# RWKV features in 30 turns, one for each 128 features of a stage, between those of latent attention

## The chip, the core and the metric

The kernel runs on one core of a Trainium2 chip. The metric is the device time of one execution in microseconds; three executions of the kernel before took 3229.11, 3230.69 and 3238.85 us, median 3230.69. Five engines work at once, each on its own queue of instructions in program order: PE (TensorE: matrix products and transposes), DVE (VectorE), ACT (ScalarE), POOL (GpSimd) and SP (SyncE, which issues the DMAs). They wait for each other only through semaphores written out in the code.

## The reference

Two blocks of two layers each on 512 tokens of width 1024, all in float32. The first block (sliding window, forgetting and mLSTM mixers, squared ReLU) is not touched. A layer of the second block computes three mixers from one projection: stick-breaking attention, latent attention (MLA, 4 heads) and RWKV-7 (8 heads of 64, 512 features), then an output projection, a norm, a feed-forward part with a short convolution, and a norm. The change lies in what the RWKV mixer does before its recurrence:

```
kk = (k * k_k).reshape(b, s, RWKV_HEADS, HEAD_DIM)
kk = kk * lax.rsqrt(jnp.maximum(jnp.sum(jnp.square(kk), axis=-1, keepdims=True), 1e-12))
k = k * (1.0 + (a - 1.0) * k_a)
...
def step(state, inp):
    sa = jnp.einsum('bhvk,bhk->bhv', state, -kk_t)
    state = (state * w_t[:, :, None, :] + sa[..., None] * (kk_t * a_t)[:, :, None, :]
             + v_t[..., None] * k_t[:, :, None, :])
    return state, jnp.einsum('bhvk,bhk->bhv', state, r_t)
...
bonus = jnp.sum(rh * kh * r_k, axis=-1, keepdims=True) * vh
```

## The kernel before

**The mixer stage.** In each of the two RWKV layers, after the input projection, all engines run the same set of strands by `turns`: each strand is a generator, and one turn calls each of them once, in the order `latent`, `stick`, `strand(2)`, `strand(3)`, `features`, `prep(0)` to `prep(3)`, `scan`, `post(0)` to `post(3)`. What a strand issues in its part of a turn goes to the engine's queue in that order. Each engine has its own generators with the same names, and their `yield`s are counted so that the same step falls into the same turn on every engine. Nothing waits at the end of a turn; a turn only fixes the order in each queue. Order between strands is set by `flags`: a strand that finds its flag missing yields and asks again next turn. A fence of all engines ends the stage, and the output projection follows.

**The strands.** `latent` makes queries and keys of latent attention and sets `mla`. `strand(2)` and `strand(3)` then work through four attention units each (`attend`, L637, L1378, L2061; 512, 384, 256, 128 keys wide, two heads each): scores on PE in a unit's turn 0, mask and maximum on DVE in 1, the negated maximum in 2, exponentials on ACT in 3, transposes on PE and their copies in 4, products with the values in 5, the scaled output on DVE in 6, so seven turns for a unit. `features` (PE L893, DVE L1703, ACT L2235, POOL L2523) makes what the recurrence needs from receptance, key, value, decay and rate, which lie as features x tokens in four chunks of 128 features by 512 tokens (`rF`, `kF`, `vF`, `KKv`, `AAv`). Its first two turns (rates and decay projections) come when stick-breaking ends; the rest when `mla` is set, in these steps, each for all four chunks in one turn: cumulative log decays (PE) and their exponentials `E1v`, `E2v` (ACT); squares of the gained key (ACT) summed by head with `Oblk` (PE); clamp at 1e-12 (DVE); reciprocal root as ln, exp (ACT) and one Newton step (DVE); values turned to tokens (PE, ACT); norm of the key, gate by `ka`, bonus operand (DVE); `AAv` times key and `E2v` (POOL); the bonus sums with `hsel` (PE); decayed key and receptance (DVE); key, normed key and rate turned (PE, copied by ACT or DVE to `KT`, `AT`, `BT`). In banks 0 to 3 of PSUM chunk c always uses bank c.

**After the features.** `prep(t)` (PE L962) inverts a triangular matrix for each tile of 128 tokens by five levels of 64x64 products and takes 17 turns on PE; `prep(0)` and `prep(1)` wait for `feat`, `prep(2)` and `prep(3)` also for the end of both attention strands (`gates_of`, L474), whose PSUM banks and buffers they use. `scan` carries the state from tile to tile. `post(t)`, the group norm, bonus and gate of a tile, waits for the states of its pair of tiles and the end of attention (`gates_post`).

In the trace nearly all DVE, ACT and POOL operations stand on lines of small helpers: L1204 tensor_tensor, L1208 and L1209 tensor_scalar, L1212 scalar_tensor_tensor, L1215 reduce, L1943 activation, L1939 activation with a sum, L2449 POOL tensor_tensor; L519 is a product and L522 a transpose of PE, L989 and L1039 products inside `prep`. Buffers are slices of larger ones: R, SC, HA and LN hold the mixer's tensors, RAW the attention scores, PS is PSUM, PSM the parameters by feature. `own(x)` issues x and waits on the engine for its end.

## Time and profile before

| | |
|---|---|
| median of three runs | 3230.69 us (3229.11 to 3238.85) |
| the profiled execution: whole time, span | 3235.39 us, 3233.6 us |
| mean granted clock of PE, as a share of 2.4 GHz | 0.916 |
| PE, DVE, ACT, POOL busy | 2880.6, 1547.8, 1044.6, 191.7 us |
| share of the span | 89%, 48%, 32%, 6% |
| DMA | 216.59 MB, 67 GB/s in the mean |

Busy time is the time in which an engine has an instruction at work. A share near 90% for PE says that the kernel as a whole is bound there, not that each stage is: the mixer stages of the second block last from 1618.5 to 1843.2 us and from 2543.7 to 2773.0 us (counted from the first scores of latent attention to the end of the mixer), and there it has to be read stage by stage. The granted clock is the share of full speed that PE was given in a stretch; its two levels are 1.2 and 2.4 GHz, so 0.72 means a mixture of both. In a timeline row stand start, length, engine, line, operation, out<-in with shapes, the count of instructions merged in it, and in brackets how long the engine had been idle and for whom.

### The profile page before, as it was taken

Reading aid. Unit: us, or ns where it says so; the run is one execution under the profiler, and the core shown is the slowest. Engines: PE = TensorE matmul, PEld = TensorE weight load, DVE = VectorE, ACT = ScalarE, POOL = GpSimd, SP = SyncE. Lnnn points to the kernel's source line nnn. Section 1 sums busy time; section 2 is a strip of 40 time slices with the busy share of each in tenths; the row PEclk is TensorE's granted clock in tenths of the full one; section 3 lists DMA queues with packets and bytes.
Section 4 is the critical chain, followed back from the end, with each engine's and each line's share of the span. In section 5 each row is a group of like instructions: output and inputs, shape, how many; then the busy total and the mean of one; then the engine's idle time right before and its main releaser. Section 6 shows DMA issues by size and latency. Waiting matters only on the chain.

```text
span 3233.6 us, 45203 instructions
## 1 busy us (share of the span) xinstructions
PE 2880.6 (89%) x19896; PEld 2379.5 (74%) x19896; DVE 1547.8 (48%) x2432; ACT 1044.6 (32%) x1554; POOL 191.7 (6%) x182
## 2 busy tenths in 40 slices
PE   7987999999888999998867789999888687789997
PEld 5876788878777888886557678888666387678885
DVE  3585533345565443424365554444533555554435
ACT  3333322232333322224232233223433432232323
POOL 0200000001100000000023200000000123000000
PEclk9977999999868999999878889999898798889998
DMA  4101222222003222221000123232210000223221
GB/s 163 53 1 62 80 103 94 102 78 84 9 1 108 99 98 98 89 86 40 1 1 29 51 89 108 92 104 78 84 52 1 1 3 29 92 78 104 91 98 46
DMA packets 30725, 216.59 MB, mean 67 GB/s; under 512 B 3648, under 2 KB 3776, under 8 KB 6080
## 3 DMA queue, kind: packets, MB, share of 16 engines
q1 hardware_dynamic: 30528, 213.69, 18.8%
q8 instruction: 157, 2.57, 0.3%
q14 instruction: 40, 0.33, 0.0%
HBM read 211.58 MB, written 2.10 MB: 66 GB/s over the span
## 4 chain that ended last, share of the span: by engine, by line
PE 80%; DVE 14%; ACT 4%; issue 2%; DMA 0%; DVEq 0%; SPq 0%; ACTq 0%
PE PS L519 76%; PE PS L522 3%; DVE SC L1204 2%; DVE SM L1215 1%; DVE X L1204 1%; DVE SM L1204 1%; DVE R L1204 1%; ACT LN L1943 1%; ACT SPL L1943 1%; DVE SPL L1204 1%; DVE HA L1204 1%; PE PS L1039 0%; PE PS L989 0%; ACT R L1943 0%; DVE SM L1209 0%
## 5 line engine op out<-in xcount | busy, mean ns | idle before, releaser
L519 PE MATMUL PS<-H,SPL 128*128 128x512 f32 (+1 forms) x4560 | 1056.4, 392 | 8.7 <-DVE SPL L1204 5.6
L519 PEld LDWEIGHTS PS<-H,SPL 128*128 128x128 f32 (+1 forms) x4560 | 853.5, 188 | 194.8 <-issue 8.2
L1204 DVE TENSOR_TENSOR SPL<-RAW,SPL 128x2048 fp32r<-128x2048 f32 (+2 forms) x194 | 434.3, 2240 | 768.3 <-ACT SPL L1943 768.3
L1943 ACT ACTIVATE SPL<-RAW 128x2048 fp32r<-128x2048 f32 (+2 forms) x194 | 362.0, 1869 | 922.4 <-PE PS L519 888.2
L519 PE MATMUL PS<-SPL,Uu 128*128 128x512 f32 x2592 | 589.8, 389 | 0.0
L519 PEld LDWEIGHTS PS<-SPL,Uu 128*128 128x128 f32 x2592 | 486.5, 188 | 101.0
L519 PE MATMUL PS<-SPL,H 128*128 128x512 f32 (+2 forms) x2112 | 463.6, 381 | 25.7 <-DVE SPL L1204 25.0
L519 PEld LDWEIGHTS PS<-SPL,H 128*128 128x128 f32 x2112 | 389.3, 193 | 99.4 <-issue 27.1
L1943 ACT ACTIVATE R<-PS 128x512 f32<-128x512 f32 (+2 forms) x182 | 104.6, 585 | 267.9 <-PE PS L519 243.1
L1204 DVE TENSOR_TENSOR X<-X,PS 128x512 f32<-128x512 f32 x112 | 76.7, 685 | 116.0 <-PE PS L519 116.0
L1943 ACT ACTIVATE Uu<-R 128x512 fp32r<-128x512 f32 x108 | 68.3, 632 | 141.2 <-DVE R L1204 141.2
L1204 DVE TENSOR_TENSOR Uu<-R,Uu 128x512 fp32r<-128x512 f32 x108 | 74.8, 693 | 79.8 <-ACT Uu L1943 79.8
L1204 DVE TENSOR_TENSOR R<-R,PS 128x512 f32<-128x512 f32 (+1 forms) x86 | 57.6, 670 | 105.5 <-PE PS L519 90.1
L519 PEld LDWEIGHTS PS<-R,SC 64*64 64x64 f32 (+1 forms) x1280 | 89.8, 182 | 19.7 <-issue 12.4
L522 PE MATMUL PS<-CST,R 128*128 128x128 f32 (+1 forms) x384 | 63.5, 332 | 41.3 <-DVE R L1208 23.4
L519 PE MATMUL PS<-R,SC 64*64 64x64 f32 (+1 forms) x1280 | 96.7, 269 | 2.4 <-ACT SC L1943 1.9
L519 PE MATMUL PS<-SM,CST 128*128 128x128 f32 (+5 forms) x224 | 61.9, 428 | 35.1 <-DVE SM L1204 35.1
L522 PEld LDWEIGHTS PS<-CST,R 128*128 128x128 f32 (+1 forms) x384 | 56.2, 173 | 49.2 <-issue 15.5
L1204 DVE TENSOR_TENSOR LN<-LN,PS 128x512 f32<-128x512 f32 (+3 forms) x74 | 42.5, 578 | 92.7 <-PE PS L519 92.6
L519 PE MATMUL PS<-R 64*64 64x64 f32 (+2 forms) x1760 | 71.7, 235 | 16.3 <-DVE R L1204 9.5
L519 PEld LDWEIGHTS PS<-SM,CST 128*128 128x128 f32 x224 | 44.1, 238 | 56.7 <-DVE SM L1204 37.9
L2449 POOL TENSOR_TENSOR HA<-HA,CST 128x64 f32<-128x64 f32 x16 | 4.6, 322 | 1313.4 <-ACT HA L1943 1313.4
(220 smaller groups left out, 2704.5 us busy)
## 6 DMA issues: line engine op xcount, KB each, us to landing
RAW<-in_wA SPq DMA_DIRECT2D x84, 1024.0 KB, 4.8
RAW<-in_wB SPq DMA_DIRECT2D x84, 1024.0 KB, 4.8
RAW<-in_wAo SPq DMA_DIRECT2D x8, 1024.0 KB, 4.8
RAW<-in_wBo SPq DMA_DIRECT2D x8, 1024.0 KB, 6.3
LN<-in_ln SPq DMA_DIRECT2D x4, 1024.0 KB, 6.1
P<-in_pB SPq DMA_DIRECT2D x2, 1920.0 KB, 8.9
RAW<-in_wBm SPq DMA_DIRECT2D x4, 704.0 KB, 4.1
X<-in_x SPq DMA_DIRECT2D x4, 512.0 KB, 5.0
```

Of the source, the lines that this page charges most:

```text
L519: return pe.matmul(out, l_, r_, start=start, stop=stop)
L522: return pe.transpose(out, i, C("ident"))
L1204: return v.tensor_tensor(out, a, b, o)
L1215: return v.tensor_reduce(out=out, in_=a, op=o, axis=AX.X)
L1943: return a.activation(out, in_, f, scale=scale)
L2449: return g.tensor_tensor(out, a, b, o)
```

## The change

After `mla` the features' steps run one chunk in a turn. Each step for all four chunks, one turn long before, becomes four turns long; the seven turns of PE after `mla` become 28, and with the two earlier ones 30. The strands on DVE, ACT and POOL get the same number of turns, with idle ones where they have nothing to do. `flags["feat"]` is set at the end of the 28th turn after `mla` on every engine, in the same turn as the last output of attention's fourth unit.

The gained key (`kF` times `kk`) is no longer written to `KKv` beforehand by four DVE operations. ACT squares `kF` with `kk` as its scale, and the norm multiplies `kF`, `kk` and the reciprocal root in one scalar_tensor_tensor. The Newton step is three operations there, not four: y times (1.5 - 0.5 x y y) is formed with two scalar_tensor_tensor and one tensor_tensor. So DVE has four operations up to the normed key in each chunk where it had five. The counts of the semaphore `fe_d` go down from 16 to 12 in a layer.

```diff
@@ -912,36 +912,38 @@
                         ins = mm(bank(c)[:, t * 128:(t + 1) * 128], LW[:, t * 512 + c * 128:t * 512 + (c + 1) * 128],
                                  C("Ublk"))
                     ins.then_inc(s.fe_p, 1)
-                yield
+                    yield
                 for c in range(4):
                     pe.wait_ge(s.fe_e, 12 * l + 4 + c + 1)
                     mm(bank(c), C("Oblk"), FT[c][0]).then_inc(s.fe_r, 1)
-                yield
+                    yield
                 for c in range(4):
-                    pe.wait_ge(s.fe_d, 16 * l + 4 + c + 1)
+                    pe.wait_ge(s.fe_d, 12 * l + c + 1)
                     turned(c, vF, c, s.fe_t)
-                yield
+                    yield
                 for c in range(4):
                     pe.wait_ge(s.fe_c, 12 * l + c + 1)
-                    pe.wait_ge(s.fe_d, 16 * l + 8 + c + 1)
+                    pe.wait_ge(s.fe_d, 12 * l + 4 + c + 1)
                     for t in range(4):
                         ins = mm(bank(c)[:, t * 2:t * 2 + 2], FT[c][0][:, t * 128:(t + 1) * 128], C("hsel"))
                     ins.then_inc(s.fe_r, 1)
-                yield
+                    yield
                 for c in range(4):
                     pe.wait_ge(s.fe_k, 8 * l + c + 1)
                     turned(c, kF, c, s.fe_t)
-                yield
+                    yield
                 for c in range(4):
                     pe.wait_ge(s.fe_c, 12 * l + 4 + c + 1)
                     pe.wait_ge(s.fe_k, 8 * l + 4 + c + 1)
                     turned(c, KKv, c, s.fe_r)
-                yield
+                    yield
                 for c in range(4):
-                    pe.wait_ge(s.fe_d, 16 * l + 12 + c + 1)
+                    pe.wait_ge(s.fe_d, 12 * l + 8 + c + 1)
                     pe.wait_ge(s.fe_g, 4 * l + c + 1)
                     turned(c, AAv, c, s.fe_t)
-                pe.wait_ge(s.fe_d, 16 * l + 16)
+                    if c < 3:
+                        yield
+                pe.wait_ge(s.fe_d, 12 * l + 12)
                 pe.wait_ge(s.fe_c, 12 * l + 12)
                 flags["feat"] = True
                 yield
@@ -1704,9 +1706,6 @@
                 while "sb" not in flags:
                     yield
                 v.wait_ge(s.par, 16 * (3 + l))
-                for c in range(4):
-                    ts(KKv[:, c, :], kF[:, c, :], par(PS, PSM, f"kk_{l}", c, c + 1), None, ALU.mult,
-                       None).then_inc(s.fe_d, 1)
                 yield
                 for t in range(4):
                     v.wait_ge(s.fe_p, 8 * l + t + 1)
@@ -1714,40 +1713,45 @@
                 yield
                 while "mla" not in flags:
                     yield
-                yield
+                for c in range(4):
+                    yield
                 for c in range(4):
                     v.wait_ge(s.fe_r, 12 * l + c + 1)
                     ts(FT[c][0], bank(c), 1e-12, None, ALU.max, None).then_inc(s.fe_d, 1)
-                yield
+                    yield
                 for c in range(4):
                     T1_, T2_, T3_ = FT[c]
                     v.wait_ge(s.fe_e, 12 * l + 8 + c + 1)
-                    own(newton(T2_, T1_, T3_))
-                    own(tt(KKv[:, c, :], KKv[:, c, :], T2_, ALU.mult))
+                    own(stt(T3_, T2_, -0.5, T2_, ALU.mult, ALU.mult))
+                    own(tt(T3_, T3_, T1_, ALU.mult))
+                    own(stt(T2_, T3_, 1.5, T2_, ALU.add, ALU.mult))
+                    own(stt(KKv[:, c, :], kF[:, c, :], par(PS, PSM, f"kk_{l}", c, c + 1), T2_, ALU.mult, ALU.mult))
                     v.wait_ge(s.rw_a, 4 * l + c + 1)
                     own(ts(T1_, AAv[:, c, :], -1.0, par(PS, PSM, f"ka_{l}", c, c + 1), ALU.add, ALU.mult))
                     own(stt(kF[:, c, :], T1_, 1.0, kF[:, c, :], ALU.add, ALU.mult))
                     stt(T1_, rF[:, c, :], par(PS, PSM, f"rk_{l}", c, c + 1), kF[:, c, :], ALU.mult,
                         ALU.mult).then_inc(s.fe_d, 1)
-                yield
+                    yield
                 for c in range(4):
                     v.wait_ge(s.fe_r, 12 * l + 4 + c + 1)
                     v.tensor_copy(BN.rearrange("p (t c g) -> p c t g", t=4, c=4)[:, c], v3(bank(c, 8), 4))
                     tt(kF[:, c, :], kF[:, c, :], E2v[c], ALU.mult).then_inc(s.fe_k, 1)
                     tt(rF[:, c, :], rF[:, c, :], E1v[c], ALU.mult)
                     v.tensor_copy(AC4[:, c, :].unsqueeze(2), E1v[c].rearrange("p (i s) -> p i s", s=64)[:, :, 63:64])
-                yield
+                    yield
                 for c in range(4):
                     e8 = E1v[c].rearrange("p (i s) -> p i s", s=64)
                     kk8 = KKv[:, c, :].rearrange("p (i s) -> p i s", s=64)
                     v.wait_ge(s.fe_h, 4 * l + c + 1)
                     tt(kk8[:, :, 1:64], kk8[:, :, 1:64], e8[:, :, 0:63], ALU.mult).then_inc(s.fe_k, 1)
-                yield
+                    yield
                 for c in range(4):
                     v.wait_ge(s.fe_r, 12 * l + 8 + c + 1)
                     v.tensor_copy(AT.rearrange("p (t c d) -> p c t d", t=4, c=4)[:, c],
                                   v3(bank(c), 4)).then_inc(s.fe_d, 1)
-                yield
+                    yield
+                for c in range(3):
+                    yield
                 flags["feat"] = True
                 yield
 
@@ -2231,6 +2235,7 @@
                     a.wait_ge(s.fe_t, k + c + 1)
                     act(dst.rearrange("p (t c d) -> p c t d", t=4, c=4)[:, c], v3(bank(c), 4),
                         ACT.Copy).then_inc(s.fe_c, 1)
+                    yield
 
             def features(l):
                 while "sb" not in flags:
@@ -2249,24 +2254,29 @@
                 while "mla" not in flags:
                     yield
                 for c in range(4):
-                    a.wait_ge(s.fe_d, 16 * l + c + 1)
-                    act(FT[c][0], KKv[:, c, :], ACT.Square).then_inc(s.fe_e, 1)
+                    act(FT[c][0], kF[:, c, :], ACT.Square,
+                        scale=par(PS, PSM, f"kk_{l}", c, c + 1)).then_inc(s.fe_e, 1)
                 for c in range(4):
                     a.wait_ge(s.fe_p, 8 * l + 4 + c + 1)
                     act(E1v[c], bank(c), ACT.Exp, scale=-DECAY)
                     act(E2v[c], bank(c), ACT.Exp, scale=DECAY).then_inc(s.fe_e, 1)
-                yield
-                yield
+                    yield
                 for c in range(4):
-                    a.wait_ge(s.fe_d, 16 * l + 4 + c + 1)
+                    a.wait_ge(s.fe_d, 12 * l + c + 1)
                     rsqrt0(FT[c][1], FT[c][0], FT[c][2]).then_inc(s.fe_e, 1)
-                turned(VT, 12 * l)
-                yield
-                yield
-                turned(KT, 12 * l + 4)
-                yield
-                yield
-                turned(BT, 12 * l + 8)
+                    yield
+                yield from turned(VT, 12 * l)
+                for c in range(4):
+                    yield
+                yield from turned(KT, 12 * l + 4)
+                for c in range(4):
+                    yield
+                for c in range(4):
+                    a.wait_ge(s.fe_t, 12 * l + 8 + c + 1)
+                    act(BT.rearrange("p (t c d) -> p c t d", t=4, c=4)[:, c], v3(bank(c), 4),
+                        ACT.Copy).then_inc(s.fe_c, 1)
+                    if c < 3:
+                        yield
                 flags["feat"] = True
                 yield
 
@@ -2527,17 +2537,16 @@
                 yield
                 while "mla" not in flags:
                     yield
-                yield
-                yield
+                for c in range(8):
+                    yield
                 for c in range(4):
-                    g.wait_ge(s.fe_d, 16 * l + 8 + c + 1)
+                    g.wait_ge(s.fe_d, 12 * l + 4 + c + 1)
                     tt(AAv[:, c, :], AAv[:, c, :], KKv[:, c, :], ALU.mult).then_inc(s.fe_h, 1)
                     g.wait_ge(s.fe_h, 4 * l + c + 1)
                     tt(AAv[:, c, :], AAv[:, c, :], E2v[c], ALU.mult).then_inc(s.fe_g, 1)
-                yield
-                yield
-                yield
-                yield
+                    yield
+                for c in range(15):
+                    yield
                 flags["feat"] = True
                 yield
 
```

## Rows read from the trace of the kernel before

**Rows 1.** The page: its first line, and section 4 by engine.

```profile
span 3233.6 us, 45203 instructions
...
PE 80%; DVE 14%; ACT 4%; issue 2%; DMA 0%; DVEq 0%; SPq 0%; ACTq 0%
```

**Rows 2.** Busy time by stage: start:end, length, PE, PEld, DVE, ACT, POOL (count), clock, DMA.

```profile
1618.50:1679.10 60.60, 35.80 (x192) 29.24 (x192) 45.86 (x72) 22.44 (x45) 13.05 (x8) 0.72 0.00 0
1679.10:1751.10 72.00, 64.83 (x1936) 60.29 (x1936) 32.53 (x66) 24.13 (x56) 21.39 (x18) 0.98 0.02 4
1751.10:1823.00 71.90, 54.31 (x1853) 51.58 (x1854) 38.65 (x62) 14.64 (x27) 27.95 (x22) 0.83 0.09 32
1823.00:1843.20 20.20, 6.09 (x116) 3.27 (x112) 15.50 (x31) 2.69 (x7) 4.90 (x4) 0.71 0.00 1
...
2543.70:2604.30 60.60, 35.67 (x195) 29.15 (x195) 45.86 (x72) 22.37 (x44) 13.06 (x8) 0.72 0.00 0
2604.30:2678.00 73.70, 65.53 (x1926) 60.30 (x1928) 32.22 (x64) 24.13 (x56) 21.43 (x18) 0.95 0.02 4
2678.00:2752.80 74.80, 57.41 (x1867) 54.35 (x1865) 39.35 (x64) 14.64 (x28) 27.95 (x22) 0.82 0.09 31
2752.80:2773.00 20.20, 6.12 (x117) 3.30 (x111) 15.49 (x31) 2.69 (x7) 4.91 (x4) 0.76 0.00 1
```

**Rows 3.** Timeline of DVE in a chunk of features; columns as told above.

```profile
1648.15 2.36 DVE L1204 TENSOR_TENSOR HA<-HA 128x512 f32<-128x512 f32 x2
1650.55 1.37 DVE L1209 TENSOR_SCALAR HA<-HA 128x512 f32<-128x512 f32 x1
...
1652.67 0.69 DVE L1204 TENSOR_TENSOR SC<-SC,HA 128x512 f32<-128x512 f32 x1
1653.40 0.48 DVE L1209 TENSOR_SCALAR HA<-SC,PSM 128x512 f32<-128x512 f32 x1
...
1654.65 0.75 DVE L1212 SCALAR_TENSOR_TENSOR HA<-R,PSM 128x512 f32<-128x512 f32 x1
```

**Rows 4.** Timeline of POOL in the same chunk, the first of its two.

```profile
1648.31 1.66 POOL L2449 TENSOR_TENSOR SC<-SC 128x512 f32<-128x512 f32 x1 [3.85 <-DVE HA L1212]
```

**Rows 5.** Timeline of PE from the first scores of latent attention on.

```profile
1618.57 5.40 PE L519 MATMUL PS<-SC 96*128 96x512 f32 x8 [4.20 <-ACT SC L1943]
1623.81 3.73 PE L519 MATMUL PS<-CST,R 128*128 128x128 f32 x32
...
1664.42 3.43 PE L522 MATMUL PS<-CST,RAW 128*128 128x128 f32 x16
...
1670.94 3.76 PE L519 MATMUL PS<-SC,RAW 128*128 128x64 f32 x32 [0.77 <-DVE RAW L1418]
...
1682.79 2.20 PE L519 MATMUL PS<-SC 96*128 96x384 f32 x6 [0.71 <-issue]
...
1695.08 1.10 PE L519 MATMUL PS<-HA,R 64*64 64x64 f32 x32
...
1751.11 2.09 PE L519 MATMUL PS<-SC 64*64 64x64 f32 x128
...
1778.15 1.92 PE L519 MATMUL PS<-HA,R 64*64 64x64 f32 x32
```

**Rows 6.** Timeline of DVE and of ACT, attention unit 1.

```profile
1630.19 1.22 DVE L1215 TENSOR_REDUCE SM<-RAW 128x2 f32<-128x1024 f32 x1
...
1640.54 0.74 ACT L1939 ACTIVATE RAW<-RAW,SM 128x512 f32<-128x512 f32 x1
```

**Rows 7.** Chain that ended last, preps 2 and 3 and post: start, length, what.

```profile
1782.99 29.64 PE PS L519 x960
...
1812.69 2.57 PE PS L989 x174
...
1819.25 3.72 PE PS L1039 x128
...
1840.27 2.09 PE PS L519 x2
```

## Prediction

> **What bounds the kernel now.** I read the page first. TensorE is busy for most of the span and the chain that ended last lies 80% on PE and 14% on DVE [rows 1]; the dense products are not touched, so what counts is the mixer stage of the two RWKV layers, the only place where the changed lines run. Then the table by stage [rows 2], cut at four events of the PE timeline: first scores of latent attention (1618.5), first pair products of the RWKV preps 0 and 1 (1679.1), those of preps 2 and 3 (1751.1), end of their last products (1823.0), end of the mixer (1843.2). I call the stretches I to IV. In I, 60.6 us, PE is busy 35.8 and DVE 45.9: the features hold everything up, one DVE chain after another. In II, 72.0 us, PE is busy 64.8: preps 0 and 1 and units 2 to 4 of attention share PE, and PE is the bound. In III, 71.9 us, PE is busy 54.3 at a mean clock of 0.83: only two preps run, and DVE is shared with the output steps (post) of tiles 0 and 1. In IV, 20.2 us, PE is nearly idle: scan, and post of tiles 2 and 3 on DVE. Sum 224.7 us in the first RWKV layer, 229.3 in the second.
>
> What sets these stretches is the turn in which a strand may start. Attention has 4 units of 7 turns on both of its strands, turns 0 to 27. Features now end in turn 6, so preps 0 and 1 (17 turns) run in 6 to 22 beside attention; preps 2 and 3 need the end of attention and run in 28 to 44.
>
> **The change part by part.**
>
> **DVE operations.** A chunk loses one operation of five in the norm of the keys (square, times sum, affine, times r, times key become four, and the multiply by the key gain is folded in). The row for the affine step undisturbed is not among the five; the tensor_scalar that gates the key took 0.48 [rows 3], so 4 x 0.48 = 1.9 us leave each layer's DVE chain. The four multiplies that made the gained key earlier stood under PE's and ACT's work before stretch I, where DVE had nothing to do; they are worth nothing, and if that cover were gone they would be 4 x 0.48 = 1.9 us.
>
> **The new turns.** Features take 28 turns after latent attention is open, 0 to 27, one 128-feature chunk in each. Attention ends in 27 as before. So preps 0 and 1 start in turn 27 and preps 2 and 3 in 28: all four together. Stretch II disappears as a stretch; the stage becomes A (turns 0 to 27: attention and features), B (27 to 44: four preps), C (scan and four posts). Posts need the states of both tiles of a pair: tiles 0 and 1 have them in turn 47, tiles 2 and 3 in turn 52, where now the first pair starts in 28 and the second in 48.
>
> *A, walked along the new order from 1618.5.* (1) To the first DVE norm chain. Scores 5.4 [rows 5], first cumulative product 0.9 (a quarter of 3.73, [rows 5]), then ACT does the exponentials of chunk 0 before it copies the scores, which queue behind that new wait: 1.8. DVE masks and reduces twice, 3.4 (1.22 each for the maximum, [rows 6]), ACT's exponentials 2.8 (4 at the 0.74 row, less their overlap, [rows 6]), transposes of the second strand 1.7 (half of 3.43, [rows 5]), sum product 0.9, value products 3.8 [rows 5], the next sum product 0.9 and the two outputs of the unit 1.1, scores of unit 2 between 2.2 and 4.4 (the row at full clock is 2.20, [rows 5]; twice that at half), I take 3.1, sum product, clamp, ln and exp, copy of the scores 3.6, small ones 0.7. Together 30.1. (2) Masks of unit 2, 2.8; four norm chains. One chain is now 4 x 0.69 + 0.75 x 2 + 0.48 plus gaps = 4.9 undisturbed [rows 3]. In the trace a chunk takes 7.2 (its last operation ends at 1655.4, that of the chunk before at 1648.2, [rows 3]), because its second and third operations wait for GpSimd's two multiplies (2.36 for two and 1.37, where alone they would take 0.69 each and about the 0.48 of the other tensor_scalar) [rows 3, 4]: 2.1 us lost in each. GpSimd still does the same two multiplies a chunk later, beside the next chunk's chain. No row has a scalar_tensor_tensor beside a GpSimd operation, so the loss is between 0 and 2.1, and could be a little more since a tiny maximum negation now stands first and waits as well; I take 2.1, as the nearest rows are tensor operations with two operands in SBUF like these. 4.9 + 3 x 7.0 + 1.5 + copies 0.9 + 2.8 = 31.1. (3) Bonus copies, decays of key and receptance, unit 3's mask, shifted keys: 16.4, DVE nearly all of it. (4) Values of unit 3, output, scores, mask, exponentials, transposes, values of unit 4 and the last turned copies: PE, DVE and ACT hand to each other, 13.9. A = 91.5, between 82 (no loss to GpSimd, -6.3, and PE at full clock, -3) and 99 (half clock throughout, +7).
>
> One rule of the Trainium skill speaks to the open price in (2): GPSIMD Engine Reference, section Specifications, says that GpSimd shares its SBUF interfaces with VectorE and collides with a VectorE operation that reads two SBUF operands, without an exception for a kind. By that the new operations lose as the old ones do (A near 91.5); by the lower end of the rows A would be 85.
>
> *B.* A prep on PE: the first products, 128 records of a pair in 2.09 [rows 5]; the second and third steps, 192 records at that pace, 2.8; the fourth, 128 records of which 32 step on by 0.94 (the row says 1.10 to their end, [rows 5]), 3.8; 960 records in 29.64; then 2.6, short ones of about 1.1, and 3.7 [rows 7]. That is 46.0 for a pair, 92.0 for four. Holes: at the start DVE has to mask for four preps (15 operations of 0.69 in the first turns, from the 0.69 row) and PE waits about 5; at the end about 2.5 (now 2.9: from 1815.3 to 1819.3 less the short ones, [rows 7]); and 1.5 for the half clock at the start. B = 101, between 96 and 106. DVE per level is 8 x 0.69 = 5.5 against PE's 11.9, GpSimd less: neither takes over. This is where the change gains: II and III are 143.9 now, A beyond I and B together 30.9 + 101 = 131.9, so 12.0 less.
>
> *C.* Scan needs tiles in order. Three steps remain after B (2.3), then post of tiles 0 and 1, then three scan adds (1.3), then post of tiles 2 and 3. A pair of posts alone is DVE after DVE and a last gate product of 2.09 at half clock [rows 7]: stretch IV less its scan, 16.7, and 17.1 with the one copy that tile 0 has. C = 37.7 against 20.2: 17.5 us more. Posts of tiles 0 and 1 are not free today, but PE fills much of their time in III; afterwards nothing is left to run beside them, since all preps are over. That is the price of the late features.
>
> **Sum.** A + B + C = 91.5 + 101 + 37.7 = 230.2 us per layer; now 224.7 and 229.3: +5.5 and +0.9, together +6.4 us. The profiled execution has a span of 3233.6 and a whole time of 3235.4, 4.7 above the median of 3230.7, within the shown runs; I put the difference on the median: 3237.
>
> **The rivals.**
>
> *Faster: the chunks fill the holes better than I walk it.* For it: stretch I has 24.8 us without PE work, III 17.6, and these are what the new order mixes. Against it: C. If the chains lose nothing to GpSimd (-6.3 per layer), PE stays at full clock in A (-3) and B has only 2 us of holes (-6), a layer is 214.9: -9.8 and -14.4, 3206.5; half way from my sum to it is 3222.
>
> *Slower: PE runs at its lower level through A.* In A PE is busy about half of the time, in bursts with idle stretches of up to 10 us. The trace has the pattern: III starts after a long idle of PE, its mean clock is 0.83, and 32 small products there take 1.92 where the same form in II, under continuous load at 0.98, takes 1.10 [rows 2, 5]. If the scores, transposes and values of units 1 to 4 all run at 1.2 GHz and the start of B too, +7 in A and up to +5 in B: a layer is 242.2, +17.5 and +12.9, 3261; half way to it from my sum is 3249. It decides against the change as soon as it costs more than 2 us per layer beyond my sum. The Trainium skill has this as its own warning, TensorE: Matmul & The Clock Gate, section on HAM oscillation: short products between waits lose the full clock again and again. The trace agrees (0.72 in I).
>
> *No effect where it is meant:* features could be bounded by attention's units anyway, and preps 2 and 3 are gated by the end of attention before and after. Then only the order of preps 0 and 1 and their posts moves, and gain in B and loss in C cancel: 3231. This is the middle of "same" and differs from my forecast by less than a measurement can tell.
>
> **How the numbers follow.** A measurement of this kernel tells about 0.3%, 9.7 us, from no change: the bounds are 3221 and 3240.4. My forecast with the no-effect case, 3221 to 3240: 0.41. Faster case: 0.24, two thirds of it between 3210 and 3221. Slower case: 0.35, two thirds of it up to 3252. The range that leaves 2 in 10 out is 3211 to 3254; it takes A between 82 and 99 nearly whole in both layers. The likeliest case's own range is 3221 to 3240.
>
> **What would show it.** In the new profile: the first pair products of preps 0 and 1 follow the values of attention's last unit, some 91 us after the first scores, and those of preps 2 and 3 come within 10 us after them. PE is busy over 90% of some 100 us from there. DVE's norm chain has four operations before the key, near 7 us a chunk when GpSimd runs. After the last prep products there are two runs of post, about 38 us to the end of the mixer, not 20. I am wrong if the chain beside GpSimd takes 5 us a chunk, if the clock in A is above 0.9 or below 0.6, if tile 0's post starts before the last prep ends, or if B has more than 10 us of idle PE.

## Result, and the profile of the changed kernel

The changed kernel takes 3260.04 us (median of 7 runs, 3248.08 to 3269.72), the kernel before 3235.11 us (7 runs, 3220.08 to 3239.17): ratio 1.0099, 95% interval 1.0071 to 1.0127. It is slower by 24.9 us. The forecast was 3237 with a range of 3211 to 3254: the result lies outside it. The profiled execution took 3267.71 us with a span of 3265.9, 32.3 more than that of before [rows 1].

The page of the changed kernel, its first line and section 4 by engine, which answer to [rows 1]:

```profile
span 3265.9 us, 45193 instructions
...
PE 81%; DVE 12%; ACT 4%; issue 2%; DMA 0%; DVEq 0%; SPq 0%; ACTq 0%
```

The table by stage of the changed kernel, both RWKV layers, cut where the prediction cut it: A from the first scores to the first pair products, B to the end of the last products of the preps, C to the end of the mixer. The columns are those of [rows 2]: start:end, length, PE, PEld, DVE, ACT, POOL, clock, DMA.

```profile
1621.50:1715.80 94.30, 61.26 (x288) 51.22 (x289) 54.54 (x100) 33.92 (x78) 12.35 (x8) 0.65 0.01 3
1715.80:1825.60 109.80, 96.78 (x3607) 94.96 (x3609) 44.26 (x65) 25.57 (x43) 44.02 (x36) 0.94 0.06 21
1825.60:1863.40 37.80, 14.16 (x202) 8.06 (x198) 30.71 (x62) 4.79 (x13) 10.05 (x8) 0.61 0.00 1
2564.00:2657.90 93.90, 60.61 (x288) 50.34 (x289) 54.55 (x100) 33.86 (x78) 12.36 (x8) 0.67 0.01 3
2657.90:2766.90 109.00, 96.53 (x3606) 94.86 (x3608) 44.13 (x65) 25.69 (x43) 43.95 (x36) 0.94 0.06 22
2766.90:2804.60 37.70, 14.51 (x200) 8.05 (x196) 30.70 (x62) 4.79 (x13) 10.05 (x8) 0.67 0.00 1
```

Beside the old stretches (I, II+III and IV in [rows 2]) and the forecast:

| us | I, II+III, IV before (layer 1; layer 2) | forecast A, B, C | after (layer 1; layer 2) |
|---|---|---|---|
| A | 60.6; 60.6 | 91.5 | 94.3; 93.9 |
| B | 143.9; 148.5 | 101 | 109.8; 109.0 |
| C | 20.2; 20.2 | 37.7 | 37.8; 37.7 |
| sum | 224.7; 229.3 | 230.2 | 241.9; 240.6 |

The two stages grew by 17.2 and 11.3 us, 28.5 of the 32.3 between the two profiled executions; 2.9 more lie ahead of the first scores, where of the change only the four removed VectorE multiplies stood; the first scores of the other profiled kernels come anywhere from 1599.5 to 1628.2 us, so this part is spread. So the place is right and C is right; A is 2.8 and 2.4 us too long, and B 8.8 and 8.0, which is most of the error.

The chain that ended last, in B of the changed kernel (start, length, what; "issue" is time in which PE waits for nothing that the profile shows):

```profile
1715.81 4.64 PE PS L519 x160
1720.45 1.47 issue
1721.92 3.45 PE PS L519 x124
1725.37 0.71 issue
1726.08 2.09 PE PS L519 x128
1728.17 1.91 issue
1730.09 2.09 PE PS L519 x127
1732.18 1.96 issue
1734.13 10.66 PE PS L519 x351
...
1799.77 2.09 PE PS L991 x128
1801.86 1.65 issue
...
1813.10 1.65 issue
```

Here stands the row from which the prediction made its price: 128 records in 2.09 us, the same as in [rows 5]. Behind such bursts stands what it left out, a pause of up to 2 us in which no engine is waited for. Eight such pauses on this chain in B add up to 10.9 us (the six shown, and 1.03 and 0.48 in the left-out part). Only one pause over 1 us in B has a releaser, 1.39 us for VectorE at 1744.77.

B of the changed kernel once more, cut into its levels (middle) and what lies behind and ahead of them:

```profile
1734.13:1799.77 65.64, 63.97 (x2168) 63.55 (x2169) 26.92 (x40) 16.72 (x28) 22.45 (x18) 0.97 0.02 4
1799.77:1825.60 25.83, 20.52 (x896) 19.68 (x898) 6.02 (x10) 6.46 (x11) 7.54 (x8) 1.00 0.02 4
1715.80:1734.13 18.33, 12.28 (x543) 11.74 (x543) 11.31 (x16) 2.39 (x4) 14.04 (x10) 0.75 0.27 107
```

Length by count gives 30.3 ns a record in the levels, 28.8 behind them, 33.8 ahead of them (where the clock is 0.75). The three are nearly alike, but not for the same reason. In the levels PE has hardly a pause: from 1747 to 1799 two products start every 59 ns, 29.5 ns for each. Outside them the 128 of a burst start 16 ns apart, and the pause makes up the rest. The levels of before had 960 in 29.64 us, 30.9 ns [rows 7].

### The profile page after: what moved, and what is told of

It reads as the page before. It is cut to its first block, busy times and chain, and to the rows that moved or that the text cites. A ratio compares the mean times of both kernels' runs of the same rounds, so it can differ in the third digit from the quotient of the medians.

```text
span 3265.9 us, 45193 instructions
## 1 busy us (share of the span) xinstructions
PE 2902.4 (89%) x19896; PEld 2399.8 (73%) x19896; DVE 1538.9 (47%) x2416; ACT 1045.9 (32%) x1554; POOL 189.8 (6%) x182
## 4 chain that ended last, share of the span: by engine, by line
PE 81%; DVE 12%; ACT 4%; issue 2%; DMA 0%; DVEq 0%; SPq 0%; ACTq 0%
PE PS L519 77%; PE PS L522 3%; DVE SC L1206 2%; DVE SM L1217 1%; DVE X L1206 1%; DVE SM L1206 1%; ACT SPL L1947 1%; ACT LN L1947 1%; DVE SPL L1206 1%; DVE R L1206 1%; PE PS L991 1%; DVE HA L1214 1%; PE PS L1041 0%; DVE X L1211 0%; DVE SM L1211 0%
## 5 line engine op out<-in xcount | busy, mean ns | idle before, releaser
L519 PE MATMUL PS<-SPL,H 128*128 128x512 f32 (+2 forms) x2112 | 462.7, 381 | 25.5 <-DVE SPL L1206 24.7
L519 PEld LDWEIGHTS PS<-R 64*64 64x64 f32 (+1 forms) x1760 | 63.1, 146 | 26.0 <-issue 12.8
```

The lines of the kernel that those rows point to most:

```text
L519: return pe.matmul(out, l_, r_, start=start, stop=stop)
```

## The experiments

A, B and C of a kernel are its stretches as in the table above, and of two numbers for one stretch the first is that of the first RWKV layer. Each stretch comes from one profiled execution. How far such a number can be trusted is seen where kernels share the lines of a stretch: A is 94.3 in the first layer and 93.6 to 93.9 in the second in the changed kernel and in three others with the same A, but B lies between 106.0 and 109.8 in four kernels with the same preps, and II+III between 143.5 and 148.5 in four with the old ones. So a difference of 2 or 3 us in B or in II+III tells nothing by itself.

**1. The two parts apart.** First the new operations in the old order of turns:

```diff
-                    own(newton(T2_, T1_, T3_))
-                    own(tt(KKv[:, c, :], KKv[:, c, :], T2_, ALU.mult))
+                    own(stt(T3_, T2_, -0.5, T2_, ALU.mult, ALU.mult))
+                    own(tt(T3_, T3_, T1_, ALU.mult))
+                    own(stt(T2_, T3_, 1.5, T2_, ALU.add, ALU.mult))
+                    own(stt(KKv[:, c, :], kF[:, c, :], par(PS, PSM, f"kk_{l}", c, c + 1), T2_, ALU.mult, ALU.mult))
```

> The kernel before with the new VectorE operations alone (no gained key beforehand, four operations up to the normed key where there were five); the turns are those of before. Theory (the cost lies in the order of the turns): stretch I of the layer, 60.6 us before, loses 4 x 0.45 to 4 x 0.75, that is 1.8 to 3 us, the rest stays, so 4 to 6 us less for the whole kernel, too little to be clear beside its spread. Rival (the new operations are the cost, because each waits longer beside GpSimd): stretch I grows, and the kernel is 10 us or more slower than before.

Measured: 3232.79 us beside 3230.64, ratio 1.0007 (0.9990 to 1.0025), no difference that can be told. Stretch I takes 59.0 and 59.4 us, 1.6 and 1.2 less than before, a little under the 1.9 of the prediction and the 1.8 expected at least; the whole layers take 226.1 and 225.9 where before has 224.7 and 229.3, no clear change.

Then the new turns with the old operations (the diff above turned round, on the changed kernel):

> The changed kernel with the old VectorE operations: only the 30 turns are kept. Theory (order of the turns): the whole loss of the change and a little more, a layer of 243 to 247 us against 224.7 to 229.3 before and 241 to 242 in the changed kernel, the kernel 28 to 38 us slower than before. Rival (the new operations are the cost): within 10 us of before.

Measured: 3256.26 us, ratio 1.0084 (1.0053 to 1.0115). A 92.9 and 92.5, B 106.0 and 109.6, C 37.6 and 37.7. So the order of the turns is the loss, and the operations are next to nothing. The layer takes 236.6 and 239.8 us, where 243 to 247 was expected: with the new operations A is 1.4 us longer than with the old ones, not shorter, and what does it stays open.

**2. The two runs of output steps.** Preps 2 and 3 wait eight turns more, on all four engines that have them:

```diff
+                if t >= 2:
+                    for _ in range(8):
+                        yield
```

> The changed kernel, but preps 2 and 3 begin 8 turns later on every engine, so the posts of tiles 0 and 1 (turn 47) fall beside the last prep turns of tiles 2 and 3 (turns 36 to 52) again. Theory (two runs of post one after another with nothing beside them cost 17.7 us a layer): the end stretch after the last prep products falls from 38 to about 20 us, the prep stretch grows from 109 to about 116 us for its lonely first and last turns, a layer about 231 us, the kernel 15 to 25 us faster than the changed one. Rival (PE's low clock and the features' own chain in turns 0 to 27 are what costs, and the preps are slow by themselves): the prep stretch grows by as much as the end shrinks, 242 us or more a layer.

Measured: 3250.88 us, ratio 1.0074 (1.0050 to 1.0099). B and C in the table by stage, first layer (A is 94.3 as in the changed kernel):

```profile
1707.50:1827.00 119.50, 102.92 (x3690) 99.40 (x3692) 58.22 (x96) 27.66 (x49) 49.60 (x40) 0.93 0.05 20
1827.00:1847.30 20.30, 6.16 (x118) 3.34 (x115) 15.49 (x31) 2.69 (x7) 4.91 (x4) 0.72 0.00 1
```

C falls from 37.8 to 20.3, the time of the old stretch IV: the 17.5 us were the second run of output steps with nothing beside it. B takes on 9.7, and DVE's work there goes from 44.3 to 58.2 us, which is that run moved beside products. Net 7.8 us a layer, not the 11 expected; the interval of the whole time overlaps that of the changed kernel (1.0071 to 1.0127), so it is the stretches that show the effect.

**3. Half way.** Two chunks to a turn instead of one, so that the features take 14 turns and preps 0 and 1 start in the middle of attention:

```diff
-                    yield
+                    if (c + 1) % 2 == 0:
+                        yield
```

> The changed kernel with two chunks of features in a turn: 14 turns after latent attention is open, so preps 0 and 1 begin in turn 13 beside attention's units 3 and 4, and their posts fall beside preps 2 and 3 as before. Theory (what costs is that all four preps start together and late): turns 0 to 13 about 75 us, then 58 with preps 0 and 1, 68 with preps 2 and 3, 20 at the end, 221 us a layer, the kernel between 10 us faster than before and the same. Rival (chunks spread between attention are slow by themselves): 230 us or more a layer, 10 us or more slower than before.

Measured: 3237.09 us, ratio 1.0023 (1.0003 to 1.0043). A 72.0 and 71.1, B 136.6 and 137.2, C 20.3, sum 228.9 and 228.5 where 221 was expected. B gets 7.3 and 11.3 us shorter than the old II and III, and A 11.4 and 10.5 longer than I: in the first layer that is less than A took, in the second a little more. C stays short, since the preps no longer all end together.

**4. GpSimd beside the norm chain.** GpSimd's two multiplies of a chunk wait for the last chunk's norm, so that no chain has them beside it:

```diff
-                    g.wait_ge(s.fe_d, 12 * l + 4 + c + 1)
+                    g.wait_ge(s.fe_d, 12 * l + 8)
```

> The changed kernel with GpSimd's multiplies held back until all four norm chains are done. Theory (VectorE's chains, stretched by GpSimd, pace A): chain period 4.9 instead of 6.9 us, A from 94 to 88 to 90 us. Rival (A is paced by hand-overs): chain period 4.9 but A within 2 us of 94.

DVE and GpSimd in the changed kernel, one chunk (columns as in [rows 3, 4]):

```profile
1659.69 0.69 DVE L1214 SCALAR_TENSOR_TENSOR HA<-HA 128x512 f32<-128x512 f32 x1
1660.41 1.64 DVE L1206 TENSOR_TENSOR HA<-HA 128x512 f32<-128x512 f32 x1
1662.08 1.65 DVE L1214 SCALAR_TENSOR_TENSOR HA<-HA 128x512 f32<-128x512 f32 x1
...
1666.47 0.68 DVE L1214 SCALAR_TENSOR_TENSOR HA<-HA 128x512 f32<-128x512 f32 x1
...
1659.71 1.79 POOL L2459 TENSOR_TENSOR SC<-SC 128x512 f32<-128x512 f32 x1 [65.83 <-DVE HA L1214]
1661.58 1.60 POOL L2459 TENSOR_TENSOR SC<-SC,R 128x512 f32<-128x512 f32 x1
```

And DVE in the kernel with GpSimd late:

```profile
1661.53 0.69 DVE L1214 SCALAR_TENSOR_TENSOR HA<-HA 128x512 f32<-128x512 f32 x1
1662.25 0.69 DVE L1206 TENSOR_TENSOR HA<-HA 128x512 f32<-128x512 f32 x1
1662.98 0.69 DVE L1214 SCALAR_TENSOR_TENSOR HA<-HA 128x512 f32<-128x512 f32 x1
...
1666.41 0.69 DVE L1214 SCALAR_TENSOR_TENSOR HA<-HA 128x512 f32<-128x512 f32 x1
...
1678.91 0.17 DVE L1737 COPY SM<-PS 128x8 f32<-128x8 f32 x1 [1.88 <-PE PS L519]
1679.00 2.94 DVE L1206 TENSOR_TENSOR R<-R 128x512 f32<-128x512 f32 x2
```

A chunk takes 6.8 us beside GpSimd and 4.9 without it, as the prediction had it (7.0 and 4.9), and the scalar_tensor_tensor goes from 0.69 to 1.65. The rule of the Trainium skill that the prediction weighed (GPSIMD Engine Reference, section Specifications: GpSimd shares its SBUF interfaces with VectorE and collides with operations that have two SBUF inputs) holds for it too. But A is only 1.3 and 3.9 us shorter (93.0 and 90.0; the layers part at unit 3's values, 3.52 us in the first and, with the full clock coming back, 2.64 in the second), and the one time, 3260.52, does not differ from the changed kernel's: the chain then waits for PE (1.88), and GpSimd falls on the decays (2.94 for two).

A variant in which GpSimd multiplies only 8 of 512 columns, to take its work away altogether, has no measured time.

The same delay in the old order, and with two chunks to a turn:

> The kernel before with the new VectorE operations, and GpSimd's multiplies of the features held back until all four norm chains of the layer are done. Theory (each chain after the first loses 2.1 us to GpSimd's work beside it): the chain period falls from 7.0 to 4.8 us, 6 us less in stretch I; GpSimd's 12 us then lie beside the decay multiplies of VectorE, which lose 2 to 3 us; stretch I falls from 59 to 54 to 56 us, the kernel 4 to 12 us faster than before. Rival (the lost time only moves, because the shifted keys wait for GpSimd's first multiplies): stretch I stays at 59 or more, no change.

> Two chunks of features in a turn, GpSimd's multiplies held back as in the run before this one. Theory: the same 6 us of collisions leave the chains, part comes back in the later VectorE steps; A from 71.5 to 67 to 69 us, B and C as they were (137 and 20), a layer 225 us, the kernel 0 to 8 us faster than before. Rival: GpSimd's last multiply now comes too late for the turned rates, A stays at 71 or grows, the kernel 5 us or more slower than before.

Measured: 3240.19 us, 1.0029 (1.0006 to 1.0052), stretch I 65.0 instead of 59; and 3236.0 us, 1.0006 (0.9982 to 1.0031), A 69.3 and 69.1, sum 228.9 and 228.2. The 54 to 56 us and the gain expected in the old order did not come: the norms end 5.7 us earlier in the stretch than with the new operations alone, but the decays behind them, now beside GpSimd's eight multiplies, take 13.9 us instead of 7.4, so that the last values start 0.7 us later, not earlier. The rest of the 6 us is the clock: it is at 0.50 there, and these values and the turned rates take 7.06 and 5.70 us, where it is 3.76 and 3.84 at the full one. (GpSimd itself is done 1.4 us before the last values start; nothing waits for it at the end.)

**5. What a pair product costs.** The prediction's price was 16 ns a record, from [rows 5]. Every pair product of the preps' first three steps is issued twice (`pairs`, 640 records more in a layer):

```diff
+                            mm(bank(b0 + g)[64 * ch:64 * ch + 64, o + c * 64:o + (c + 1) * 64], lv[rows, c, ts_],
+                               rv[rows, c, ts_])
```

> The changed kernel with every product of the first three prep steps issued twice, 640 more records of PE in a layer, of the kind that runs at 14 to 16 ns a record in a burst. Theory (PE cannot keep that pace: over a longer stretch it gets a record each 29.5 ns, whatever the form, because instructions don't arrive faster): B grows by about 19 us, from 109.4 to 128. Rival (those records cost what they take in a burst, and the gaps around them are waits for masks): B grows by 9 us or less, since part hides under the waits for VectorE.

Measured: B 125.3 and 125.8 us, 15.5 and 16.8 more: 24 to 26 ns for each added record, not 16. That is under the 19 us of the theory and far over the 9 of the rival. The chain that ended last, at the full clock, where only such products run:

```profile
1713.89 2.24 PE PS L519 x125
1716.13 1.25 issue
1717.38 2.18 PE PS L519 x124
1719.56 1.44 issue
1721.00 2.19 PE PS L519 x125
1723.18 1.71 issue
1724.89 2.54 PE PS L519 x125
```

The starts of the pieces are 3.5, 3.6 and 3.9 us apart, with 125 or so records and one pause in each: 28 to 31 ns a record. What has this step is in the DMA part of the same views. First B of the changed kernel, then B of this one (queue, kind: packets, MB, share):

```profile
q8 instruction: 28, 0.46, 1.8%
```

```profile
q8 instruction: 33, 0.54, 1.8%
```

The first is 0.46 MB for 3607 records, 128 bytes a record, 16 KB and 129 records a packet, one packet in 3.9 us. The Trainium skill (Runtime: NRT & Kernel Launch, section Instruction fetch mechanics) says that an engine's instructions are refilled in blocks of 16 KiB by the sequencer's own queue while it executes, and that the cost is mostly hidden. The block size agrees; "mostly hidden" does not hold here, where 1.2 to 2 us are visible in each 125 records. The second view has 33 packets for 4247 records, 129 records a packet again, one in 3.8 us. These counts say only that every instruction is brought in once. The times of the packets in the traces say more. B of both layers has 11 pauses over 0.8 us without a releaser between such products in the changed kernel and 24 in this one; each of the 11 ends 1.30 to 1.57 us after a packet of 16 KB has landed, each of the 24 1.20 to 1.49 us after. Packets come only every 3.4 to 4.5 us, so ends that had nothing to do with them would lie anywhere in that time. In the piece shown the next packet starts 1.1 us after PE has gone on, takes 1.0 to 1.4 us, and PE goes on 1.2 to 1.5 us after it: these are the steps of 3.5 to 3.9 us. In the levels 128 products take 3.8 us by their own pace, and there no pause is seen, though the packets come as often. So PE waits for its instructions in the pauses, as far as times can show it; no run here changes the refill alone.

One other cause of the pauses could be separated. At the start of B, 1.9 MB of weights arrive by DMA; here they wait for the third result of prep 1:

```diff
+                        sp.wait_ge(s.pr_q[1], 9 * l + 3)
```

> The changed kernel, but the 2 MB of weights that are loaded when attention ends (0 to 5 us after the first pair products) are held back until prep 1 is in its first level. Theory (that load delays the instruction fetch of PE): the gaps without a releaser on PE in the first 20 us of B, 6.0 us, fall by 2 us or more, and B with them, 109 to 107 or less. Rival (they have nothing to do with it): B stays within 1 us.

Measured: B 108.4 and 109.2 us beside 109.8 and 109.0, one time of 3267.45. The pauses without a releaser in the first 20 us of B are 4.1 and 3.7 us instead of 6.0 and 5.4: the first of them is shorter, those of 1.6 to 2 us stay. So the weights do not make the pauses; whether they lengthen the first one stays open, and B shows no gain beyond its spread.

**6. The low clock.** The granted clock in A is 0.65 and 0.67. Extra products are put into PE's pauses there, and overwritten before anyone reads them. First two runs with them in turns 10 and 11 only (70 and 60, then 44 and 36):

```diff
+                    if c == 2:
+                        pe.wait_ge(s.fe_d, 12 * l + 4)
+                        for _ in range(44):
+                            mm(bank(3, 128), C("ident"), C("ones"))
```

> The changed kernel with 130 products added to PE in turns 10 and 11, whose result is overwritten before anyone reads it: they fill PE's two long idle stretches (10.7 and 9.1 us) in A. Theory (PE's lower clock in A costs time): the clock stays high from the values of unit 2 on, scores of unit 3 take 2.2 instead of 3.8 us, A falls by 4 to 7 us and the start of B by 2 to 3. Rival (VectorE covers PE's slow work): PE's pieces shorten but A changes by less than 2 us.

> The changed kernel with 80 extra products on PE in turns 10 and 11 where the run warm had 130, which held the values of unit 2 back by some 7 us: these end just before the next real product. Theory (PE's low clock in A costs time that is not hidden): A falls from 94 to 87 to 90 us. Rival (the clock is hidden behind VectorE): A stays at 92 to 94.

Measured: 3258.48 and 3259.13 us (one time each), A 92.4 and 92.1 with the many, 94.4 and 93.9 with the few, B 108.2 and 110.4, 106.8 and 109.2. Neither answers the question: the many held real products up by some 7 us, the few ended 2.2 us before the next real product, and the clock was 0.50 again from there. Then a third run, with 44 and 46 in those turns, 7, 12 and 12 in three later pauses:

> The changed kernel with 121 extra matrix products in turns 10, 11, 13, 17 and 24 of each stage's walk, whose results are overwritten before anyone reads them; they fill TensorE's idle stretches from unit 2's decay work to the first pair products, so that the granted clock need not fall there. Outputs are unchanged. Theory (the low clock in the first part costs time of its own): granted clock near 1.0 to the first pair products, unit 3's score groups 2.2 us instead of 3.8, the first part 86 to 90 us instead of 94, and 2 to 3 us less in the stretch of the pair products, since it starts at the full clock. Rival (the low clock is hidden behind VectorE's decay work): the first part 92 to 94 us with the clock up, and at most 2 us less in the pair products.

Its first two stretches, and PE in three places of A:

```profile
1621.50:1710.70 89.20, 77.86 (x531) 68.29 (x531) 54.83 (x100) 33.47 (x78) 12.81 (x8) 0.89 0.01 2
1710.70:1818.10 107.40, 93.35 (x3607) 91.29 (x3609) 44.93 (x65) 25.54 (x43) 43.79 (x36) 0.98 0.06 23
```

```profile
1673.97 2.86 PE L519 MATMUL PS<-SC,RAW 128*128 128x64 f32 x24
1676.67 1.90 PE L519 MATMUL PS<-CST,HA 128*128 128x2 f32 x16
...
1697.96 2.00 PE L519 MATMUL PS<-SC,RAW 128*128 128x64 f32 x16
```

The same three in the changed kernel:

```profile
1673.86 5.36 PE L519 MATMUL PS<-SC,RAW 128*128 128x64 f32 x24 [9.08 <-DVE RAW L1420]
1679.01 3.52 PE L519 MATMUL PS<-CST,HA 128*128 128x2 f32 x16
...
1698.81 3.52 PE L519 MATMUL PS<-SC,RAW 128*128 128x64 f32 x16
```

Measured: A 89.2 and 88.7, 5.1 and 5.2 us less; B 107.4 and 107.8, 2.4 and 1.2 less; one time of 3250.87. The clock went from 0.65 to 0.89, and the values of units 2 and 3 and the bonus sums take 0.53 to 0.57 of their time. (The scores of unit 3 still took 3.78, after a pause of 4.06 us that was not filled; there the expectation missed.) So the low clock costs 5 us in A in the new order. The 2.4 and 1.2 us in B lie within its spread, and experiment 7 does not bear them out. Nor does all of the faster work pay. The first two rows shown gain 2.5 and 1.6 us for PE, and the scores of unit 3 come 62.8 us after the first scores instead of 62.9, since VectorE's decays stand between; the 5 us are won behind them, in units 3 and 4. The warning in the Trainium skill (TensorE: Matmul & The Clock Gate, section HAM oscillation) fits it: short products between waits run at the low clock.

The old order's stretch I runs at 0.72 [rows 2] as well. Does it pay the same price? Extra products between the bonus sums of the four chunks there, and in two of the runs also behind the first products of preps 2 and 3:

```diff
                     pe.wait_ge(s.fe_c, 12 * l + c + 1)
+                    for _ in range((7, 21, 21, 21)[c]):
+                        mm(bank(c, 128), C("ident"), C("ones"))
                     pe.wait_ge(s.fe_d, 16 * l + 8 + c + 1)
```

> The kernel before with 214 extra matrix products in each RWKV layer, whose results are overwritten or never read: 16, 24, 40 and 40 in TensorE's pauses beside the four norm chains of stretch I, and 94 behind the first products of preps 2 and 3. Outputs are unchanged. Theory (the low clock costs more in the new order than in the old one, because in stretch I of the old order it lies under VectorE's chain): the granted clock goes up in I and at the start of III, stretch I gets at most 2 us shorter (transposes 3.4 to 1.9 us), III at most 3, a layer 1 to 4 us, the time 3223 to 3229 beside a before of 3231. Rival (the low clock costs the old order as much as the new one): 5 us or more in I alone, 14 us or more in all, below 3217.

> The kernel before with extra matrix products again, 114 in each RWKV layer: 7, 21, 21 and 21 beside the norm chains of stretch I and 44 behind the first products of preps 2 and 3. In the run with 214 of them each took 0.23 us at the full clock and not 0.11, so that they overran the pauses (9.2 us where the pause is 5.3) and held VectorE up; these fit the pauses. Outputs are unchanged. Theory (in the old order the low clock of stretch I lies under VectorE's chain): stretch I goes from 60.6 to 58 or 59 us, the start of III gets at most 3 us shorter, the time 3222 to 3231 beside a before of 3231. Rival (the low clock costs the old order as much as the new one): stretch I at 55.5 us or less, the time below 3217.

> The same with only the 70 extra products of stretch I in each layer, none behind the first products of preps 2 and 3; it tells the two places apart. Theory: stretch I 58 to 59 us, stretches II to IV as before, the time 3226 to 3231. Rival: stretch I at 55.5 us or less, the time near 3221 or below.

The first had products too many: 40 of them took 9.2 us in a pause of 5.3, stretch I became 64.4 us, the ratio 1.0072 (1.0043 to 1.0101); it measured the overrun. The second gave 1.0039 (1.0021 to 1.0057), slower too: its products behind those of preps 2 and 3 held more up than they gave (II+III 150.7 and 150.3 instead of 143.9 and 148.5, and stretch I took 60.6 and 63.8). The 3.2 us of its second layer are not lost beside the norms, although a group of 21 ran there partly at the low clock: up to the last values it keeps step with the others, and these values and the turned rates then fall into a stretch of low clock (3.76 and 3.84 us at the full one):

```profile
2596.34 4.62 PE L519 MATMUL PS<-SC,RAW 128*128 128x64 f32 x32 [0.78 <-DVE RAW L1432]
2600.75 6.15 PE L522 MATMUL PS<-CST,SC 128*128 128x128 f32 x32
```

There PE is on the path, and a low clock is paid in the old order too, as in the kernel with late GpSimd of experiment 4 (5.2 us). The kernel before has the full clock at that place. The third is the clean one: 3235.84 us beside 3232.09, ratio 1.0003 (0.9987 to 1.0020). Its stretch I, and the part of it beside the norm chains:

```profile
1620.00:1680.60 60.60, 51.90 (x332) 44.89 (x332) 45.88 (x72) 22.50 (x44) 13.07 (x8) 0.86 0.00 1
1644.70:1665.00 20.30, 18.97 (x151) 18.64 (x152) 19.61 (x26) 0.24 (x2) 8.59 (x6) 0.91 0.00 1
```

The clock went from 0.5 to 0.91 beside the norms, and stretch I stayed at 60.6 us in both layers. There DVE is busy 19.6 of 20.3 us, and PE's speed doesn't matter; the 2 us expected from the transposes behind the norms did not come. (The low clock was back there, transposes 3.29 us where the run with products too many had 1.95; but behind them PE waits for VectorE again, 0.69 and 0.77 us, so little is left to win.) The products leave the first 20 us of stretch I, ahead of the norms, as they were. In the new order extra products stand between attention's units, where PE, ACT and DVE hand to each other, and there the low clock costs 5 us.

**7. Do the prices add up?** The eight turns of experiment 2 and the products of the third run of 6 together:

> The changed kernel with both cures at once: the 121 extra products of the run that kept the clock up, and preps 2 and 3 eight turns later, so that only two tiles' output steps are left at the end. Theory (the two prices add up and nothing else is left that the old order does not have): first part 89 us, second 117 to 118, third 20.3, a layer 226 to 228 against 241.9 and 240.7, the time within 0.3% of the kernel before. Rival (they overlap): a layer above 230, the time at least 0.3% above before.

Measured: 3238.40 us beside 3230.77, ratio 1.0013 (0.9997 to 1.0029), within what can be told from no change. A 89.1 and 88.7, B 117.5 and 120.3, C 20.2 and 20.3, sum 226.9 and 229.3; the two single effects taken off the changed kernel say 226.6 and 226.4, so that in the second layer B is 3 us longer than they say; the kernel before has 224.7 and 229.3. Against experiment 2, which differs by the extra products alone, A is 5.2 and 4.9 us shorter, B 2.0 shorter and 1.3 longer, and the ratio falls from 1.0074 (1.0050 to 1.0099) to 1.0013 (0.9997 to 1.0029). Here the price of the low clock stands in the whole time, clear of the spread, and in the stretches it is A's. With both prices taken off, no difference between the new order and the old one can be told. No kernel here beats the one before.

## Why the prediction was wrong, point by point

**A, the features in the pauses: 91.5 forecast, 94.3 and 93.9 measured.** The walk and its chain are right: 6.8 us for a chunk beside GpSimd (forecast 7.0), 54.5 us of DVE. The mis-sized term is the clock: with the pauses filled A is 89.2 and 88.7, so the low clock costs 5.1 us, where the prediction gave "PE at full clock, -3". What is left of the difference is under 1 us. The loss beside GpSimd is written as 2.1 us a chunk, but the rows named for it give 1.9 (2.36 and 1.37, less 1.38 and 0.48), and 1.9 was measured. The lower end of the range was wrong too: with that loss gone A fell by 1.3 and 3.9 us, not by 6.3.

**B, four preps: 101 forecast, 109.8 and 109.0 measured.** This is the step that failed. "The first products, 128 records of a pair in 2.09; the second and third steps, 192 records at that pace" took the pace inside a burst for the pace of the work; behind each 125 records or so of these stands a pause of 1 to 2 us that belongs to them. The prediction saw one of them ("now 2.9: from 1815.3 to 1819.3 less the short ones") and called it a hole at the end, to be paid once. The levels were taken from 960 records at once and came out right. Four preps have some 3600 records. At the rate of the levels, 29.64 us for 960 [rows 7], they cost 111 us, 1.5 more than measured; the sum had 92.0 for them, 25.5 ns each, and 9 us of holes. By pieces: ahead of the levels 18.3 us, forecast 16.3 (9.8, 5 and 1.5); the levels and their first step 65.6, forecast 66.9; behind them 25.8, forecast 17.3 (twice 7.4, and 2.5), where some 4 us of the 25.8 are 127 products of the last level. The 5 us in which PE was to wait for VectorE's masks at the start did not come as such: PE stands idle there for 6.0 us, but for pauses without a releaser. (192 records at the named pace are 3.1 us, not the 2.8 written; with 3.1 the terms give the 46.0 of the sum.) Experiment 5 showed it with the disputed products alone: 24 to 26 ns each where 16 was claimed. In the old order the same price was paid, but it lay in stretches that were measured whole, so it never had to be priced.

**C, two runs of output steps: 37.7 forecast, 37.8 and 37.7 measured.** Right, and experiment 2 shows the mechanism: two tiles' steps taken away from the end make it 20.3. (The terms written out give 37.4.)

**The DVE operations: 1.9 us less per layer forecast, 1.6 and 1.2 measured** in the old order; not to be seen in the whole time, and not in the new order.

**The rival "slower" gave 3261 us, and 3260 was measured, but not for its reason.** It put up to 12 us a layer on the low clock (7 in A, 5 in B). The runs put 5.1 and 5.2 into A, of which the sum already held 3, and in B no more than the 1.5 that it held can be told from the spread. So about 2 us of the misses of 11.7 and 10.4 are the clock's; nearly all of the rest stands in B, as the price of the products. That 3261 came so near is luck: a clock term of 12 us a layer stood in for a price of products that it did not have. Here only the filled pauses told the two apart. The rival "faster" fell with B: its 2 us of holes were 13 us of idle PE. (Taking the holes from 9 to 2 would have been 7 us, where it has 6.) The rival "no effect" was refuted by the runs of experiment 1.

**The signs set beforehand.** The first pair products came 94 us after the first scores (said: 91) and those of preps 2 and 3 9 to 10 us behind them (said: within 10); the norm chain 6.8 us (near 7); 37.8 us at the end (about 38); clock in A 0.65 (0.6 to 0.9). PE was busy 88% of B, not over 90%, with 13 us idle: the one condition under "I am wrong" that was met points at the step that failed.

**The chances.** The measured ratio is beyond the range's end of 3254 by 6 us. The range carried the clock's price, but B only from 96 to 106: its upper end came from holes, and no bound was taken from the other pace that the same rows held.

## What to carry to other kernels

Price a run of many small products by the longest row of the same kind at hand, length by count over several hundred, and never by a burst: a group's own row leaves out the pause behind it. When work is moved into another engine's pauses, ask what had hidden it before and what will run alone in its place; here the moved features shortened what goes before C by 0.4 and 6.2 us (12.0 was forecast for the first layer, 16.6 for the second) and left 17.5 us of output steps alone at the end. And a low clock is paid only where TensorE is on the path: the same cure was worth 5 us in one order and nothing beside the norms of the other, where VectorE is busy throughout; at the end of that same stretch, where TensorE is on the path, a low clock cost two kernels 3.2 and 5.2 us.

## What the runs showed of the hardware beyond that

- Products of 64x64 in the preps' first three steps run at 16 ns a record for about 125 records and then pause for 1.2 to 2 us, and each pause ends 1.2 to 1.6 us after a packet of 16 KB has landed on the instruction queue; this gives 28 to 31 ns a record. In the levels the same shape starts each 29.5 ns without a pause.
- At the full clock 40 extra products of 128x128 and 128 columns took 9.2 us, 0.23 us each (two records each); 21 took 4.93 us, and 6.6 where the low clock lasted for part of them. Products meant to fill a pause cost as much as they overrun it.
- The length of one pause does not tell here whether the clock falls. It was at 0.50 behind a pause of 1.33 us in stretch I of the old order with 70 extra products, but stayed at 1.00 from 1703.0 to 1822.4 us in the kernel with doubled products, through pauses of 1.2 to 1.7 us.
